# The in-projection's tiles of the head pairs taken by twos, with seven block products in place of eight

## What is computed

```python
proj = x @ w_in                                   # 512 x 1024 times 1024 x IN_COLS
pa = token_shift_mix(proj[..., :RWKV_COLS], mu)   # p + (previous token's p - p) * mu
r, k, v = ...                                     # 512 columns each, 8 heads of 64
o_a = rwkv7_branch(r, k, v, wl, al, gl, ...)      # decay, normalised keys, wkv7_scan over the tokens
o_b = sgu_branch(proj[..., OFF_SGU:OFF_CONV], ...)
o_c = conv_branch(proj[..., OFF_CONV:OFF_GATE], ...)
gates = sigmoid(proj[..., OFF_GATE:IN_COLS])      # 3 x 1024 columns
merged = gates[:, :D] * o_a + gates[:, D:2*D] * o_b + gates[:, 2*D:] * o_c
x = layer_norm(ALPHA * x + merged @ w_out, ln1_g, ln1_b)
x = layer_norm(ALPHA * x + grouped_moe(x), ln2_g, ln2_b)
```

## Time and profile before

| | us |
|---|---|
| median of three runs | 1075.15 (1074.27 to 1075.35) |
| the profiled execution | 1076.2, its span 1074.2 |
| first product to the head pairs' loop | 6 to 106 |
| the four head pairs | 106 to 454 |
| output products, mix, norm, router | 454 to 595 |
| experts | 595 to 1074 |

### The profile page before, as it was taken

One profiled execution on the slowest core, in us unless ns is written; L12 is line 12 of the kernel. 1 busy time (PEld: TensorE's weight loads), 2 busy tenths in 40 slices (PEclk: granted clock), 3 DMA queues, 4 the chain that ended last, 5 costly groups with the idle time before them and its releaser, 6 DMA issues.

```text
span 1074.2 us, 17631 instructions
## 1 busy us (share of the span) xinstructions
PE 977.5 (91%) x6604; PEld 432.9 (40%) x6605; DVE 474.2 (44%) x1053; ACT 289.5 (27%) x474; POOL 226.8 (21%) x336
## 2 busy tenths in 40 slices
PE   7999999999999999799998888888888888887774
PEld 3644455455455446344444333333333333322221
DVE  0696453564463364422328333444434444443333
ACT  1114322322322133100014233333333333322322
POOL 2000010010010010023124233333333333332322
PEclk9999999999999999999999999999999999999998
DMA  9432311221220220472946999999999999999992
GB/s 286 122 79 59 79 41 42 64 55 41 59 59 24 59 59 3 162 275 117 396 172 220 377 412 416 391 417 416 415 416 414 416 415 415 415 414 417 416 400 103
DMA packets 96900, 256.68 MB, mean 239 GB/s; under 512 B 17484, under 2 KB 62540, under 8 KB 72016
## 3 DMA queue, kind: packets, MB, share of 16 engines
q1 hardware_dynamic: 85024, 240.57, 58.8%
q0 software_dynamic: 11024, 13.20, 3.7%
q10 hardware_dynamic: 800, 2.15, 0.5%
HBM read 260.66 MB, written 21.23 MB: 262 GB/s over the span
## 4 chain that ended last, share of the span: by engine, by line
PE 52%; DMA 17%; issue 9%; DVE 7%; SPq 7%; POOL 5%; ACT 2%; POOLq 1%; ACTq 0%; DVEq 0%
PE proj L1464 12%; DMA y_rows<-const,raw 12%; PE proj L1423 11%; SPq L506 7%; PE bank L1640 5%; PE proj L1651 5%; PE bank L1566 4%; PE bank L1780 3%; DMA xT_sb<-w_gu 3%; DMA pass_sb<-x_rows,raw 2%; POOL pass_sb L578 2%; POOL const L595 2%; PE proj L1431 1%; PE bank L1801 1%; PE proj L1442 1%
## 5 line engine op out<-in xcount | busy, mean ns | idle before, releaser
L1464 PE MATMUL proj<-xT_sb,ring 128*128 128x512 f32 x384 | 185.7, 611 | 0.0
L1780 PE MATMUL bank<-arena 128*64 128x512 f32 x544 | 122.8, 596 | 19.5 <-DMA arena<-w_gu 10.7
L1423 PE MATMUL proj<-xT_sb,ring 128*128 128x512 f32 (+1 forms) x272 | 119.1, 594 | 0.0
L1347 DVE TENSOR_TENSOR const<-bank,const 128x512 f32<-128x512 f32 x33 | 22.8, 691 | 161.2 <-DMA const<-y_rows,raw 161.2
L1464 PEld LDWEIGHTS proj<-xT_sb,ring 128*128 128x128 f32 x384 | 66.9, 189 | 63.0 <-issue 59.2
L1780 PEld LDWEIGHTS bank<-arena 128*64 128x64 f32 x544 | 42.3, 136 | 99.8 <-issue 81.2
L1423 PEld LDWEIGHTS proj<-xT_sb,ring 128*128 128x128 f32 (+1 forms) x272 | 50.8, 188 | 64.6 <-issue 64.5
L852 ACT ACTIVATE pass_sb<-bank 128x256 f32<-128x256 f32 x33 | 12.7, 384 | 199.2 <-PE bank L1780 199.2
L1780 PE MATMUL bank<-gates,arena 128*64 128x512 f32 x256 | 57.4, 596 | 7.9 <-PE bank L1801 4.1
L1640 PE MATMUL bank<-branches,arena 128*128 128x512 f32 x128 | 58.0, 615 | 6.3 <-DVE branches L1106 6.3
L595 POOL DMA_INDIRECT const<-y_rows,raw x33 | 34.7, 1052 | 124.8 <-DMA y_rows<-const,raw 124.0
(11 more groups left out here) (310 smaller groups left out, 1334.8 us busy)
## 6 DMA issues: line engine op xcount, KB each, us to landing
arena<-w_gu SPq DMA_DIRECT2D x64, 1024.0 KB, 25.1
gates<-w_gu SPq DMA_DIRECT2D x32, 1024.0 KB, 23.6
arena<-w_down SPq DMA_DIRECT2D x24, 1024.0 KB, 26.7
ring<-w_in SPq DMA_DIRECT2D x42, 512.0 KB, 3.9
gates<-w_down SPq DMA_DIRECT2D x16, 1024.0 KB, 25.5
xT_sb<-w_gu SPq DMA_DIRECT2D x16, 1024.0 KB, 27.0
branches<-w_down SPq DMA_DIRECT2D x16, 1024.0 KB, 27.4
ring<-w_gu SPq DMA_DIRECT2D x16, 1024.0 KB, 25.9
```

The source lines that it names most:

```text
L1423: ins = pe.matmul(proj[0:w, b, :], ring[:, slot, k, 0:w], xT_sb[:, k, :], start=(k == 0), stop=(k == KT - 1))
L1464: ins = pe.matmul(proj[:, gate_at["bank"], :], ring[:, gate_at["slot"], k, :], xT_sb[:, k, :], start=(k == 0), stop=(k == KT - 1))
L1780: ins = pe.matmul(bank[SLOTS * h:SLOTS * h + SLOTS, 0, :], xeT[:, k % 4, SLOTS * (k // 4):SLOTS * (k // 4) + SLOTS], gu[k // 2][:, k % 2, ...
```

## The change

The 32 tiles of the head pairs (12 raw, 20 gate tiles) become 16 pairs of tiles, four per head pair: (r, k), (v, gate), (gate, gate), (gate, gate). For a pair, the weights are cut into halves of the contraction (a11, a12 of the first tile, a21, a22 of the second) and xT into halves of contraction and tokens (x11, x12, x21, x22). Seven block products, each of 4 matmuls of 256 columns, 28 in all, take the place of eight. They need sums: those of xT are made once by GpSimd (four at the start, `x_t1` over x12 when the last early gate is done); those of the weights are made by GpSimd for every pair, five operations in `weight_sums(q)` (three of 512 columns, two of 256). The products leave in four groups, each half or all of a bank of `proj`: group 1 after matmul 7, 2 after 15, 3 after 23, 4 after 27. ScalarE copies the first product; VectorE's `join` adds each group to the outputs in SBUF; ScalarE then makes the sigmoid of a gate tile in place, of the second tile after group 3, of the first after group 4.

TensorE waits inside `fill_pairs`: at matmul 0 for the join of group 3 of the pair before, at 8 for that of its group 4, at 16 and 24 for the joins of groups 1 and 2 of its own pair, and at 4, 8 and 24 for weight sums. The order in a head pair is 28 matmuls (r, k), LoRA products, 16 matmuls, L1510's product, 12 matmuls, L1512's, and then 56 more by the new `FILL`; v's shift moves behind the scaled operands. In VectorE's program the joins stand at the places of the fills; that of `FILL["var"]`, in which group 4 of the last pair ends, stands behind the wait for `s_out`. SyncE loads a pair's two slots when the pair two before is done.

In the output products' first row, the gating unit's products of rows 1 and 0 are issued before the wait for the last `s_out`.

```diff
-SOLVE_FILL = (2, 1, 1, 1, 2, 1, 1)
-FILL = {"prep": 13, "turned": 2, "scores": 3, "first": 1, "solve": sum(SOLVE_FILL), "maps": 2, "chain": 1, "y": 3, "var": 0}
+SOLVE_FILL = (3, 2, 2, 2, 2, 2, 1)
+FILL = {"prep": 16, "turned": 4, "scores": 5, "first": 1, "solve": sum(SOLVE_FILL), "maps": 3, "chain": 1, "y": 3, "var": 0}
+PLAIN, UNITS = 10 + EARLY, 28
+PAIRS = HP * (3 + PAIR_GATES) // 2
+FILL["var"] = 2 * UNITS - sum(v * {"chain": CHUNKS - 1}.get(k, 1) for k, v in FILL.items())
+class Stream:
+    ENDS = {7: 1, 15: 2, 23: 3, 27: 4}
...
+    def ended(self, n):
+        return [(u // UNITS, self.ENDS[u % UNITS]) for u in self.step(n) if u % UNITS in self.ENDS]
+def gates_of_pair(q):
+    hp, n = divmod(q, 4)
+    g = EARLY + PAIR_GATES * hp
+    return ((None, None), (None, g), (g + 1, g + 2), (g + 3, g + 4))[n]
...
+        w_s1 = pass_sb[:, 0:HK * P].rearrange("p (k m) -> p k m", k=HK)
+        w_s2 = branches[:, HP - 1, :].rearrange("p (k m) -> p k m", k=HK)
...
-                if n >= RING:
+                if n >= RING + PLAIN:
+                    sp.wait_ge(s_grp, 4 * ((n - RING - PLAIN) // 2 + 1))
+                elif n >= RING:
...
+            for n, (to, left, right) in enumerate(((x_t4, x12, x11), (x_t3, x22, x12), (x_t2, x22, x_t4), (x_t4, x21, x_t2))):
+                pool.tensor_tensor(to, left, right, SUB).then_inc(s_xsum, 1)
+                pool.wait_ge(s_xsum, n + 1)
+            def weight_sums(q):
...
+                for i in range(2):
+                    pool.wait_ge(s_win[slot + i], 16 * (turn + (slot >= 2)))
+                if q:
+                    pool.wait_ge(s_grp, 4 * q - 2)
+                pool.tensor_tensor(w_s1, a21, a22, ADD).then_inc(s_wsum, 1)
+                pool.wait_ge(s_wsum, 5 * q + 1)
+                pool.tensor_tensor(w_s2, w_s1, a11, SUB).then_inc(s_wsum, 1)
+                pool.wait_ge(s_wsum, 5 * q + 2)
+                pool.tensor_tensor(a21, a11, a21, SUB).then_inc(s_wsum, 1)
+                pool.wait_ge(s_wsum, 5 * q + 3)
+                if q:
+                    pool.wait_ge(s_grp, 4 * q)
+                for i in range(2):
+                    ks = slice(2 * i, 2 * i + 2)
+                    pool.tensor_tensor(w_s4[i], a12[:, ks, :], w_s2[:, ks, :], SUB).then_inc(s_wsum, 1)
+                    pool.wait_ge(s_wsum, 5 * q + 4 + i)
...
             for hp in range(HP):
+                if hp:
+                    weight_sums(4 * hp)
+                weight_sums(4 * hp + 1)
+                weight_sums(4 * hp + 2)
                 pool.wait_ge(s_ch, hp + 1)
...
+                weight_sums(4 * hp + 3)
...
+            def evac_pairs(n):
+                for q, group in stream.ended(n):
+                    tiles, outs = gates_of_pair(q), pair_out(q)
+                    if group == 1:
+                        act.wait_ge(s_grp, 4 * q + 1)
+                        if tiles[0] is None:
+                            act.wait_ge(s_rawfree, 2 + 3 * (q // 4) + q % 4)
+                        act.activation(outs[0][:, LO_T], proj[:, 0, LO_T], ACT.Copy).then_inc(s_c11, 1)
+                    for i, last in ((1, 3), (0, 4)):
+                        if group == last and tiles[i] is not None:
+                            act.wait_ge(s_join, 4 * q + group)
+                            act.activation(outs[i], outs[i], ACT.Sigmoid).then_inc(s_gate, 1)
...
+            def join(n):
+                for q, group in stream.ended(n):
+                    (a, b), lo, hi = pair_out(q), LO_T, HI_T
+                    dve.wait_ge(s_grp, 4 * q + group)
+                    if group == 1:
+                        dve.wait_ge(s_c11, q + 1)
+                        ins = dve.tensor_tensor(a[:, hi], a[:, lo], proj[:, 0, hi], ADD)
+                    elif group == 2:
+                        dve.wait_ge(s_join, 4 * q + 1)
+                        then(dve.tensor_tensor(b[:, lo], a[:, hi], proj[:, 1, lo], ADD))
+                        if q % 4 == 1:
+                            dve.tensor_tensor(b[:, hi], b[:, lo], proj[:, 1, hi], ADD)
+                            ins = dve.tensor_tensor(a[:, hi], a[:, hi], proj[:, 1, hi], ADD)
+                        else:
+                            both, cross = pair_views(q)
+                            ins = dve.tensor_tensor(both[:, :, hi], cross, proj[:, 1, hi].unsqueeze(1).broadcast_to([P, 2, HT]), ADD)
+                    elif group == 3:
+                        dve.wait_ge(s_join, 4 * q + 2)
+                        if q % 4 == 1:
+                            dve.tensor_tensor(a[:, lo], a[:, lo], proj[:, 0, lo], ADD)
+                            ins = dve.tensor_tensor(b[:, lo], b[:, lo], proj[:, 0, hi], ADD)
+                        else:
+                            both = pair_views(q)[0]
+                            ins = dve.tensor_tensor(both[:, :, lo], both[:, :, lo], proj[:, 0, :].rearrange("p (i t) -> p i t", i=2), ADD)
+                    else:
+                        ins = dve.tensor_tensor(a[:, hi], a[:, hi], proj[:, 1, lo], ADD)
+                    ins.then_inc(s_join, 1)
...
-                shift(v_, 8 + hp)
+                join(16)
...
                 then(dve.scalar_tensor_tensor(kkn, kk, -1.0, norm, MUL, MUL))
+                join(UNITS - 16)
...
+                dve.wait_ge(s_join, 4 * (4 * hp + 2))
+                shift(v_, 8 + hp, 0)
...
+                join(FILL["y"])
                 dve.wait_ge(s_yroot, hp + 1)
...
                 dve.wait_ge(s_out, hp + 1)
+                join(FILL["var"])
...
+            def fill_pairs(n):
+                for u in stream.step(n):
+                    q, at = divmod(u, UNITS)
...
+                    if at == 0:
+                        pe.wait_ge(s_win[slot], 16 * ((PLAIN + 2 * q) // RING + (slot >= 2)))
+                        if q == 0:
+                            pe.wait_ge(s_projfree, (12 + EARLY))
+                            pe.wait_ge(s_xsum, 4)
+                        else:
+                            pe.wait_ge(s_join, 4 * q - 1)
+                    elif at == 4:
+                        pe.wait_ge(s_wsum, 5 * q + 2)
+                    elif at == 8:
+                        pe.wait_ge(s_wsum, 5 * q + 3)
+                        if q == 0:
+                            pe.wait_ge(s_xsum, 5)
+                        else:
+                            pe.wait_ge(s_join, 4 * q)
+                    elif at == 16:
+                        pe.wait_ge(s_join, 4 * q + 1)
+                    elif at == 24:
+                        pe.wait_ge(s_wsum, 5 * q + 5)
+                        pe.wait_ge(s_join, 4 * q + 2)
...
-                parts = [(2, conv_out, 6, 2), (0, rwkv_out, 0, 4), (1, sgu_out, 4, 2)]
-                for n, src, k0, nk in parts:
+                conv, gated, heads = (2, conv_out, 6, 2), (1, sgu_out, 4, 2), (0, rwkv_out, 0, 4)
+                parts = ([(m, *conv), (1, *gated), (m, *gated), (m, *heads)] if m == 0 else
+                         [(m, *conv), (m, *heads)] if m == 1 else [(m, *conv), (m, *heads), (m, *gated)])
```

More of the change, by code:

```diff
@@ L250, in program, with pair_slot, pair_out, pair_views @@
         L16, L16T, LX, Z16T = (per_chunk(HD) for _ in range(4))
+        HT, HK = T // 2, KT // 2
+        LO_T, HI_T = slice(0, HT), slice(HT, T)
+        x11, x12, x21, x22 = (xT_sb[:, ks, ts] for ks in (slice(0, HK), slice(HK, KT)) for ts in (LO_T, HI_T))
+        x_t1 = x12
+        x_t2, x_t3, x_t4 = (cut(HK * HT, r="p (k t) -> p k t", k=dict(k=HK)) for _ in range(3))
+        w_s1 = pass_sb[:, 0:HK * P].rearrange("p (k m) -> p k m", k=HK)
+        w_s2 = branches[:, HP - 1, :].rearrange("p (k m) -> p k m", k=HK)
+        w_s4 = (pass_sb[:, HK * P:HK * P + 2 * P].rearrange("p (k m) -> p k m", k=2), cut(2 * P, r="p (k m) -> p k m", k=dict(k=2)))
+        def pair_slot(q):
+            return (PLAIN + 2 * q) % RING
+        def pair_out(q):
+            outs = []
+            for i, g in enumerate(gates_of_pair(q)):
+                outs.append(gates[:, g, :] if g is not None else raw[:, i if q % 4 == 0 else 0, 1:T + 1])
+            return outs
+        def pair_views(q):
+            if q % 4 == 0:
+                both, cross = raw[:, :, 1:T + 1], raw[:, :, :].rearrange("p i n -> p (i n)")[:, 1 + HT:3 + HT + T]
+            else:
+                g = gates_of_pair(q)[0]
+                both, cross = gates[:, g:g + 2, :], gates[:, g:g + 2, :].rearrange("p i t -> p (i t)")[:, HT:HT + T]
+            return both, cross.rearrange("p (i t) -> p i t", i=2)[:, :, LO_T]
         def over(at, n):
@@ L917, in _, with shift @@
                     ins.then_inc(s_convacc, 1)
-            def shift(dst, mu, rows_=P, done=None):
-                n = seq["raw"]
-                seq["raw"] += 1
-                ph = 10 + n if n < 2 else 12 + EARLY + (3 + PAIR_GATES) * ((n - 2) // 3) + (n - 2) % 3
-                dve.wait_ge(s_projfree, ph + 1)
-                now, before = raw[0:rows_, n % 2, 1:T + 1], raw[0:rows_, n % 2, 0:T]
+            def shift(dst, mu, n, rows_=P):
```

(15 more changed lines are left out.)

121 lines of the change are left out of this document (75 added, 46 removed).

## The result

The changed kernel took 1088.9 us (median of 4 runs, 1087.6 to 1090.1), the kernel before, beside it on the same chip, 1075.25 (1074.3 to 1077.0). The ratio is 1.0125, with a 95% interval of 1.0107 to 1.0143. The prediction was 1086.5. The profiled execution took 1090.1, its span 1088.2, against 1076.2 and 1074.2 before: 14.0 us more of span.

The account below looks back on a forecast made before the run. Heads were taken as bound by TensorE's work, with the DMA-bound expert stage passing changes on. Terms -0.2 + 6.4 + 5.1 = +11.3 us took the profiled 1076.2 to 1087.5, median 1086.5; range 1071 to 1097.

Parts of the forecast that it names:

- TensorE's work: Sixteen pairs in the heads: 28 matmuls, 12.08 us, replace two tiles' 13.74 us: -26.4 us.
- unit 0 of the first pair: First matmul of the first pair waits for ScalarE's copy of the last early gate: +0.85 us.
- wait at unit 8: Matmul 8 of the first pair in three heads waits 4.25 us for group 4's join behind s_out: +12.75 us.
- raw pair to transposes: Per head, waits of 1.6 before the third pair and 0.95 before the transposes, less 0.43 before: +8.5 us.
- solve and chain: Shorter fill under the solve and chain steps loses 1.2, 0.25 and 1.3 us per head: +11.0 us.
- end: the wait: Wait before the last head products falls from 6.26 to 2.05 us, with more products ahead: -4.2 us.
- end: the clock: Granted clock no longer at 1.2 GHz behind the wait before the last head products: -2.7 us.
- GpSimd beside VectorE: GpSimd's sums hold VectorE's SBUF operations 1.6 us per head, bounds 0 and 3: +6.4; exclusive lock would give 2.3 per head.
- clock falls in the heads: Granted clock falls at the three 4.25 us waits, 1.7 us lost each, bounds 0 and 2.7: +5.1 us.
- The rival on the other side: TensorE stays the heads' bound: 1042 with all waits gone, 1058 with half; below 1071, chance 0.12.

Follow-up runs that it names:

- sums of one column: Changed kernel with GpSimd's five weight sums per pair made on one column each, semaphores kept, weights' sums not real: 1081.5 us, ratio 1.0055.
- the kernel whose clock was kept up: Changed kernel with nine idle matmuls of 256 columns ahead of the wait before matmul 8 in heads 1 to 3: 1079.6 us, ratio 1.0053.
- the kernel before with new output products: Kernel before, without pairs, with only the order of the output products changed, gating unit's products ahead of the last s_out wait: 1072.6 us, ratio 0.997.
- the join out of its place: Changed kernel with group 4's join of each head's last pair moved ahead of VectorE's wait for y's square root: 1068.6 us, ratio 0.9941.
- the second join and the copies too: Changed kernel with last-pair and second-pair joins moved earlier in VectorE's program, and ScalarE's first solve copies ahead of the gate's sigmoid: 1062.8 us, ratio 0.9885.

## Why the prediction was right, and which of its terms were not

The time, the sign and the main mechanism were right. The terms, in the prediction's order:

| term | predicted us | measured us | from |
|---|---|---|---|
| TensorE's work | -26.4 | -26.4 | four units start to start in 1.73 us, as counted |
| unit 0 of the first pair | +0.85 | +0.73 | idle before the first unit |
| wait at unit 8 | +12.75 | +12.3 | waits, L1117 |
| raw pair to transposes | +8.5 | +7.5 | waits with sums of one column, 7.1 + 2.1 less 1.7 |
| solve and chain | +11.0 | about +11.6 | second row of the table: -12.1, predicted -12.7 with its saved work |
| end: the wait | -4.2 | -4.4 | 6.26 to 1.85 |
| end: the clock | -2.7 | -2.7 | the shortfall of 3.4 before, less 0.7 inside the wait; none after |
| GpSimd beside VectorE | +6.4 | +3.2 | 24.96 less 24.15, four heads |
| clock falls in the heads | +5.1 | about +10.8 | below |

**The wait at unit 8** was right in place, size and cause; so were the wait before the third pair (2.3 with the holds, 1.8 without them, against the 1.6 predicted) and the one at the transposes, which is 0.54 us in head 0 and gone in the heads whose products ran slowly just before. The chain's steps last 0.9 to 1.4 us, as foreseen.

**GpSimd's holds** meet the instructions that the prediction named, but also L1140, which has one SBUF input and takes 1.23 for 0.43, and they meet at 0.8 us per head on the path, not 1.6: the largest of the four stands ahead of a wait. The prediction said that the rows showed only VectorE held. The new ones show GpSimd held as well: L605 takes 0.73 and then 1.06 beside L1025 and L1026. The Trainium skill, "SBUF — State Buffer", section "SBUF: two separate sides", has an exclusive lock with which each side blocks the other; this trace agrees with that, and not with the 2.3 us per head that I worked out from it, because the path was only partly there. Two kinds of VectorE instruction went on undisturbed beside a sum: the joins that read PSUM (L1098 at 128.99, 0.42 us beside L595) and the reciprocal (3.35 us, beside L599).

**The clock** is the term that failed in size: "I take 1.7" and "bounds are 0 and the 2.7 above", for one fall in each of three heads. First, the falls at unit 8 lost more: against the kernel whose clock was kept up, 3.04 / 1.69 / 3.05, 7.8 in all. The upper bound of 2.7 was right for the fall it came from and no bound for these. In the kernel before, the same shortfall of 3.4 us began earlier against the end of its wait:

```profile
452.00:454.00 2.00, 0.00 (x0) 0.00 (x0) 1.90 (x4) 0.00 (x0) 0.00 (x0) 0.66 0.00 0
454.00:456.00 2.00, 1.86 (x2) 0.84 (x3) 0.09 (x1) 0.00 (x0) 0.00 (x0) 0.50 0.41 66
```

The clock fell at 452.65, the products began at 454.14, so 1.5 us at half clock passed in the wait and 5.3 on products. In the changed kernel only 0.7 passed in the wait. Second, there were falls that the prediction didn't have. Heads 1 to 3 have another one behind the wait of 2.3 us before the third pair, in the changed kernel's timeline:

```profile
228.97 2.85 PE L1669 MATMUL proj<-xT_sb,ring 128*128 128x256 f32 x8 [2.30 <-DVE gates L1112]
231.61 2.73 PE L1669 MATMUL proj<-arena,branches 128*128 128x256 f32 x8
```

It loses 1.7 us of work each time, and 0.99 of it stays on the path (25.95 less 24.96), as VectorE's chain to the transposes ends then. 7.8 + 3.0 = 10.8. The reason given for 1.7, that TensorE is fully busy from unit 8 on, held for one of the three falls there; the other two lost some 3.0 each.

**Two errors of opposite sign met.** The holds were 3.2 too dear, the clock 5.7 too cheap, the predicted sum 11.3 and the measured one of the table about 12.6. That the total came within 2.4 us is therefore in part luck. The difference to 14.0 is open in the main. The known parts beside the table nearly cancel: the head pairs' loop began 2.2 us later, of which 0.7 is unit 0's wait and a good part a later start of the whole kernel (the kernel before with new output products also reached the first LoRA products 0.9 us later than the kernel before, with no change ahead of them), and the expert stage was 1.9 us shorter. That leaves some 1.8 us that were not followed.

The rival on the other side, TensorE staying the bound, was wrong for this kernel but partly right about the change: with the join out of its place, the same products end 6 us ahead of the kernel before, and with the second join and the copies too, 12 to 13 us. That is below the 1071 at which I had drawn this rival's line, and far from the 1042 of all waits gone.

## What to carry to other kernels

When a product is made to wait for an evacuation, find that evacuation in the program of its engine and read everything that stands ahead of it: all three losses that could be undone here (about 20, 4 and 4 us) were instructions of 0.4 to 0.7 us in a wrong place, and adding filling across such a place only made it a new one. A shorter TensorE program spends its gain on waits first; price each wait twice, by its length and by the slow matmuls behind it, since here 12 us of waiting took 9 more in that way. Where experiments are close, compare intervals between fixed instructions of heads in which the clock did not fall, not only the medians.

## What the runs showed of the hardware beyond what I expected

- The granted clock fell to 1.2 GHz behind waits much shorter than the 6.3 us of the kernel before: behind 2.8 us at the output products, behind 2.3 in three of four heads of the changed kernel and in one of four with the join ahead, behind 1.45 in two of four. It did not do so every time: the same waits of 1.45 us with the copies ahead passed with 1.00 in every window of the one execution that has a trace.
- The shortfall was close to 1.7 us or to 3.4 in every fall of the traced heads. On the products it cost up to 1.7 us or about 3 (3.0 and 3.05 at unit 8 by the comparison with the clock kept up), because the longer falls began inside the wait.
- Nine products of 256 columns that nobody reads, put in each of three waits of 4.1 us, made the kernel 9.3 us faster.
- A VectorE instruction with one SBUF input was held by GpSimd's sums (L1140, 1.23 for 0.43 us), a reciprocal with one SBUF input was not (3.35 us with and without). Undisturbed, L1140 passes its 512 columns faster than an addition of two inputs (0.43 against 0.69 us), the reciprocal far slower.
